# One decoder layer on one core: experts 0 and 1's rows selected in turned form, a ring of six raw weight tiles, and finer last pieces

## The reference

```python
y = mixer_sublayer(x, positions, w_in, w_branch_attn, w_branch_ret, w_out)
x = layer_norm(ALPHA * x + y, ln1_scale, ln1_bias)
y = hierarchical_moe(x, ...)          # top-1 group of 4, then top-2 of its 8 experts
x = layer_norm(ALPHA * x + y, ln2_scale, ln2_bias)
...
# one expert, for the rows that were routed to it
hid = silu(xb @ w_gate[e]) * (xb @ w_up[e])     # 2048 -> 512, twice
y = hid @ w_down[e]                             # 512 -> 2048
```

## Time and profile before

| | before |
|---|---|
| median of 3 runs | 2062.95 us (2062.85 to 2064.05) |
| the profiled execution's own time | 2060.22 us |
| its span, first to last instruction | 2058.1 us |
| TensorE busy | 1766.7 us, 86% |
| VectorE busy | 994.9 us, 48% |
| ScalarE busy | 757.1 us, 37% |
| mean granted clock | 0.928 |
| read from HBM | 609.61 MB |

### The profile page before, as it was taken

One profiled execution on the slowest core, in us unless ns is written; L12 is line 12 of the kernel. 1 busy time (PEld: TensorE's weight loads), 2 busy tenths in 40 slices (PEclk: granted clock), 3 DMA queues, 4 the chain that ended last, 5 costly groups with the idle time before them and its releaser, 6 DMA issues.

```text
span 2058.1 us, 25311 instructions
## 1 busy us (share of the span) xinstructions
PE 1766.7 (86%) x9868; PEld 1141.9 (55%) x9868; DVE 994.9 (48%) x1469; ACT 757.1 (37%) x1321; POOL 15.3 (1%) x34
## 2 busy tenths in 40 slices
PE   9999999999999999999999986666566666666667
PEld 7888888888888888888888541111112111111222
DVE  5454454555444444566565564334433433343357
ACT  5444444344444444354443422222222222222221
POOL 0000000000000000000000000000000000000000
PEclk9999999999999999999999988887888888887888
DMA  7556655455556555467677999999999999999998
GB/s 247 194 175 189 199 175 176 150 184 187 191 181 194 172 185 178 155 188 238 218 279 287 381 428 425 429 431 429 427 430 433 430 426 429 431 430 427 430 428 367
DMA packets 139042, 615.07 MB, mean 299 GB/s; under 512 B 14228, under 2 KB 14900, under 8 KB 117840
## 3 DMA queue, kind: packets, MB, share of 16 engines
q1 hardware_dynamic: 138240, 611.75, 77.5%
q0 software_dynamic: 720, 2.18, 0.6%
HBM read 609.61 MB, written 2.36 MB: 297 GB/s over the span
## 4 chain that ended last, share of the span: by engine, by line
PE 54%; DMA 33%; issue 10%; DVE 2%; ACT 0%; SPq 0%; DVEq 0%; POOL 0%; POOLq 0%
DMA W<-in_w_expert_up_dram 21%; PE PS L593 14%; PE PS L595 14%; PE PS L594 14%; DMA W<-in_w_expert_down_dram 11%; PE PS L1173 5%; PE PS L1224 2%; PE PS L962 1%; PE PS L1314 0%; PE PS L1129 0%; DVE ZACC L2234 0%; PE PS L1052 0%; DMA VC<-VS 0%; PE PS L1295 0%; PE PS L939 0%
## 5 line engine op out<-in xcount | busy, mean ns | idle before, releaser
L570 DVE TENSOR_TENSOR WL<-RAW,WH 128x1024 fp32r<-128x1024 f32 x384 | 457.4, 1221 | 403.9 <-ACT WH L566 402.5
L566 ACT ACTIVATE WH<-RAW 128x1024 fp32r<-128x1024 f32 x384 | 394.5, 1058 | 261.6 <-PE PS L595 199.8
L593 PE MATMUL PS<-WH,XH 128*128 128x512 f32 x1216 | 480.0, 395 | 0.1
L595 PE MATMUL PS<-WH,XL 128*128 128x512 f32 x1216 | 474.0, 390 | 0.0
L594 PE MATMUL PS<-WL,XH 128*128 128x512 f32 x1216 | 473.3, 389 | 0.0
L1173 PE MATMUL PS<-W,XE 128*32 128x512 f32 x2016 | 277.3, 698 | 135.0 <-DMA W<-in_w_expert_up_dram 133.6
L2234 DVE TENSOR_TENSOR ZACC<-PS,ZACC 128x1024 f32<-128x1024 f32 x124 | 146.0, 1219 | 294.3 <-PE PS L1295 294.3
L1224 PE MATMUL PS<-W,HT 128*32 128x512 f32 x992 | 171.0, 851 | 135.7 <-DMA W<-in_w_expert_down_dram 135.7
L593 PEld LDWEIGHTS PS<-WH,XH 128*128 128x128 f32 x1216 | 228.3, 188 | 49.3 <-issue 1.7
L595 PEld LDWEIGHTS PS<-WH,XL 128*128 128x128 f32 x1216 | 228.2, 188 | 48.3
L594 PEld LDWEIGHTS PS<-WL,XH 128*128 128x128 f32 x1216 | 228.6, 188 | 45.8
(11 more groups left out here) (333 smaller groups left out, 1472.7 us busy)
## 6 DMA issues: line engine op xcount, KB each, us to landing
RAW<-in_w_in_dram SPq DMA_DIRECT2D x304, 512.0 KB, 4.5
W<-in_w_expert_gate_dram SPq DMA_DIRECT2D x61, 2048.0 KB, 28.6
W<-in_w_expert_up_dram SPq DMA_DIRECT2D x61, 2048.0 KB, 33.0
W<-in_w_expert_down_dram SPq DMA_DIRECT2D x28, 4096.0 KB, 35.2
RAW<-in_w_branch_ret_dram SPq DMA_DIRECT2D x32, 512.0 KB, 5.2
RAW<-in_w_out_dram SPq DMA_DIRECT2D x32, 512.0 KB, 6.0
W<-in_w_expert_down_dram SPq DMA_DIRECT2D x7, 2048.0 KB, 30.4
RAW<-in_w_branch_attn_dram SPq DMA_DIRECT2D x16, 512.0 KB, 5.3
```

The lines of the kernel that those rows point to most:

```text
L566: act.activation(WH[:, i % RING], RAW[:, i % RING], ACT.Copy).then_inc(hi_done, 1)
L570: dve.tensor_tensor(WL[:, i % RING], RAW[:, i % RING], WH[:, i % RING].bitcast(F32), ALU.subtract).then_inc(lo_done, 1)
L593: pe.matmul(PS[:, bank + t], hs, wh, start=first and j == 0, stop=False)
L595: mm = pe.matmul(PS[:, bank + t], ls, wh, start=False, stop=end)
```

## The change

1. **Selection of items 0 and 1.** `gather` and `turn_rows` are no longer used for them. `gather_turned(k)` makes, for each of the 16 channel blocks k, two products (one per token tile) with 128 columns of ZN (every eighth column) as stationary operand and both items' selections, SEL01, 64 columns, as moving operand. The result is already turned. ScalarE scales it straight to XE of both items: 16 operations of 128 x 64 in place of 32 of 128 x 32 and two copies. XG0, XG1 and SEL1 are gone.
2. **TensorE's order.** Item 0's 16 places are done one by one, with a gather_turned two places ahead between them and, in the first half, item 1's place behind each.
3. **The ring.** RAW has six places, WL is written over RAW, and the load of tile n waits for `tile_used` of tile n - 6.
4. **Last pieces.** One piece of WT0 (1 MiB) is issued behind tile 27 of the output projection; the others are of 512 KB, each waiting for a pair of tiles; W11 moves up from the end.
5. `select_next(2)` on VectorE waits for all 16 turned products (`first_turned`) in place of gather(1).

```diff
 RING = 4
+RAWS = 6
...
-    RAW = at("RAW", 32, [RING, KT, CH])
-    WH = at("WH", 48, [RING, KT, CH], F32R)
-    WL = at("WL", 64, [RING, KT, CH], F32R)
+    RAW = at("RAW", 40, [RAWS, KT, CH])
+    WL = at("WL", 40, [RAWS, KT, CH], F32R)
+    WH = at("WH", 64, [RING, KT, CH], F32R)
...
-    def load_tile(eng, tile, i, src):
-
-        eng.wait_ge(lo_done, tile + 1)
-        eng.dma_start(RAW[:, i % RING], src).then_inc(raw_landed[i % RING], 16)
+    def load_tile(eng, tile, src):
+
+        if tile >= RAWS:
+            eng.wait_ge(tile_used, tile - RAWS + 1 + RING)
+        eng.dma_start(RAW[:, tile % RAWS], src).then_inc(raw_landed[tile % RAWS], 16)
...
+    def first_place(k):
+
+        return (XE_BANK, SPREAD + 1)[k % 2], k // 2 * 2 * ROWS
...
+            if n == 27:
+                load_apart(1, 4, 8)
...
-        sp.wait_ge(lo_done, T4 - 2 + RING)
-        load_apart(1, 4, 8)
+        sp.wait_ge(tile_used, T4 - 6 + RING)
+        load_apart(0, 0, 2)
         sp.wait_ge(tile_used, T4 - 4 + RING)
-        load_apart(0, 0, 4)
-        sp.wait_ge(tile_used, T4 - 1 + RING)
-        load_apart(0, 4, 7)
-        load_apart(1, 0, 3)
+        load_apart(0, 2, 4)
+        sp.dma_start(W11[:], gate_w[:, 1, 1, 0:2 * HID]).then_inc(part_landed, 16)
+        sp.wait_ge(tile_used, T4 - 2 + RING)
+        load_apart(0, 4, 6)
+        load_apart(1, 0, 2)
         sp.wait_ge(tile_used, T4 + RING)
-        load_apart(0, 7, 8)
-        load_apart(1, 3, 4)
+        load_apart(0, 6, 8)
+        load_apart(1, 2, 4)
         for c in range(2):
             load_block(0, 2, 2, c)
-        sp.wait_ge(lo_done, T4 + RING)
-        sp.dma_start(W11[:], gate_w[:, 1, 1, 0:2 * HID]).then_inc(part_landed, 16)
...
+        def gather_turned(k):
+
+            bank, c0 = first_place(k)
+            a = k // KQ * KQ * P + k % KQ
+            for t in range(TOK):
+                mm = pe.matmul(PS[:, bank, c0:c0 + 2 * ROWS], ZN[:, t, a:a + KQ * P - k % KQ:KQ],
+                               SEL01[:, t].rearrange("p i r -> p (i r)"), start=t == 0, stop=t == TOK - 1)
+            mm.then_inc(first_turned, 1)
...
-        gather(0)
+        pe.wait_ge(sel_ready, 2 * TOK)
+        pe.wait_ge(z_norm, TOK)
+        gather_turned(0)
+        gather_turned(1)
         place_rows()
-        turn_rows(0)
-        count_rows()
-        pe.wait_ge(sel_ready, 2 * TOK)
-        gate_up(0, 0, 0, take(0), gathered_between=1)
-        gate_up(1, 1, 0, take(1))
-        gate_up(0, 0, 1, take(0))
+        for k in range(KD):
+            q, j = divmod(k, KQ)
+            gate_up(0, 0, q, take(0), places=range(j, j + 1))
+            if k == 1:
+                count_rows()
+            if k + 2 < KD:
+                gather_turned(k + 2)
+            if q == 0:
+                gate_up(1, 1, 0, take(1), places=range(j, j + 1))
         gather(2)
         gate_up(1, 1, 1, take(1))
...
+        for k in range(KD):
+            act.wait_ge(first_turned, k + 1)
+            bank, c0 = first_place(k)
+            act.activation(XE[:, :, k], PS[:, bank, c0:c0 + 2 * ROWS].rearrange("p (i r) -> p i r", i=2), ACT.Identity,
+                           bias=LSB[:, 1, k:k + 1], scale=LSB[:, 0, k:k + 1]).then_inc(
+                *((xe_first, 1) if k < KD - 1 else (xe_stored, 2 * QS)))
...
-            dve.wait_ge(gathered, item)
+            if isinstance(item, int) and item == 2:
+                dve.wait_ge(first_turned, KD)
+            else:
+                dve.wait_ge(gathered, item - 2)
```

More of the change, by code:

```diff
@@ L471, in sem @@
         return ctx.enter_context(nc.semaphore(name))
-    raw_landed = [sem(f"raw_landed{i}") for i in range(RING)]
+    raw_landed = [sem(f"raw_landed{i}") for i in range(RAWS)]
     hi_done, lo_done, tile_used = sem("hi_done"), sem("lo_done"), sem("tile_used")
@@ L1120, in gather @@
             pe.wait_ge(sel_ready, item * TOK + TOK)
[L1121 to L1125 removed]
+            pe.wait_ge(xe_stored, item * QS)
             for t in range(TOK):
@@ L1149, in gate_up @@
                 pe.wait_ge(part_landed, 16 * 6)
-            for m in range(2):
+            for m in range(2) if places[0] == 0 else ():
                 if apart:
-                    pe.wait_ge(t_landed[m], 16 * 3)
+                    pe.wait_ge(t_landed[m], 16 * (4, 3)[m])
                 elif more:
@@ L1160, in gate_up @@
                     pe.wait_ge(w_landed[pair_q][1], item * 8 + (16 * loads_until(q, k4, (0, 1)) - 8 * k4))
-            for j in range(KQ):
+            for j in places:
                 k = KQ * q + j
                 odd = j % 2
-                if by_place and j < KQ - 1:
-                    pe.wait_ge(xe_first, item * (KQ - 1) + j + 1)
+                if by_place and k < KD - 1:
+                    pe.wait_ge(xe_first, k + 1)
                 elif by_place:
-                    pe.wait_ge(xe_stored, item * QS + 1)
+                    pe.wait_ge(xe_stored, 2 * QS)
                 for m in range(2):
@@ L1178, in gate_up @@
                         pe.wait_ge(late_landed[m], 16)
-                if gathered_between is not None and j % 2 and j < KQ - 1:
+                if isinstance(item, int) and item == 0 and q == 0 and odd and j < KQ - 1:
                     mm.then_inc(gu_part, 1)
-                    if j == 3:
-                        gather(gathered_between)
-                    elif j == 5:
-                        turn_rows(gathered_between)
-            mm.then_inc(gu_used, 2)
+            if places[-1] == KQ - 1:
+                mm.then_inc(gu_used, 2)
         def turn_hidden(item):
@@ L1588, in _ @@
         for n in range(BR):
[L1589 removed]
+            split_high(act, T2 + n, n)
             if n == LAG - 1:
```

77 lines of the change are left out of this document (29 added, 48 removed).

## The result

| | before | after |
|---|---|---|
| median | 2062.85 us (5 runs, 2061.11 to 2064.05) | **2084.31 us** (5 runs, 2079.82 to 2085.28) |
| ratio to before, 95% interval | | 1.0102 (1.0091 to 1.0114) |
| the profiled execution's time and span | 2060.22, 2058.1 us | 2083.52, 2081.5 us |
| mean granted clock | 0.928 | 0.927 |

The change costs 21.5 us by the medians. The forecast was +6.3 us, 2069.2, in a range that ended at 2076. The direction was right, the size was not.

A forecast was written before the change was run, and what follows sets the result against it. Experts' stage bound by DMA bytes: item 1's down block landing +5.7 us, plus 0.6 for TensorE's later loads, gave +6.3 on the profiled 2060.2; with 2.7 to the median, 2069.2 us, range 2061.5 to 2076.

The forecast's parts named there:

- The bound and the mark: Experts' stage lasts as long as its bytes take; the landing of item 1's down block, 1186.9 us, sets the end.
- The ring of six: Raw tiles in the mixer, issued 13.5 us before TensorE needs them: bounds 0 and +3 us, taken as 0.
- the pieces: Last loads before the mixer's last tile are out of the way sooner: gain 0 to 1 us, taken as 0.7.
- A pair of the new products between two groups: TensorE's selections of items 0 and 1: 0.70 us per visit, 0.21 of it the rest of the changeover, 14 visits.
- weight loads with every eighth column: Turned products' loads, named among things that would each add 2 to 7 us; XG's step of four was 0.12 us.
- Selections ready at 1149.22: Hand-over to the experts: selections for both items ready at 1149.22 us, TensorE's turned products starting at 1149.3.
- the third rival: Worse than forecast, chance 0.14: item places not running together, +13.2 us; dear weight loads, lower clock or ring waits, 2 to 7 each.
- ScalarE hidden by TensorE's groups: ScalarE's one 128 x 64 operation per 1.56 us step takes under 1.06 us, two pairs ahead, so it adds nothing.
- The empty queue gives back 2.9 us: Item 1's down block, issued 8.6 us later into an empty DMA queue, takes 12.7 us and lands only 5.7 later.
- VectorE's wait: VectorE's later hidden(0) holds TensorE's turn_hidden(0) to 1182.3 us, though TensorE is there at 1179.6: +0.6 us on the stream.
- No price for the changeover: Rival, chance 0.24: a turned pair's visit costs only its four weight loads, 0.44 us; +2.1 us, 2065.1.
- Everything hides: Rival, chance 0.10: turned products run in the groups' shadow, a step is 0.86 us; -2 us, 2061.

The follow-up runs named there:

- the run with the wait and no fall of the clock: The changed kernel with 128 columns of z side by side, not every eighth, as the turned products' stationary operand: 2073.20 us, ratio 1.0047.
- the run with the products apart: The changed kernel with its turned products in two runs of eight places ahead of all groups of the first halves, columns still every eighth: 2079.35 us, ratio 1.0077.
- the run with both edits: The changed kernel with turned products in two runs of eight places ahead of the groups, and stationary columns side by side: 2070.47 us, ratio 1.0041.
- the two without the wait: The changed kernel with select_next(2) behind DIAG and VAL, 2079.60 us; the same with side-by-side stationary columns and each moving column twice, 2071.62 us.

## Why the prediction missed

- **The bound and the mark: right.** The experts' stage was limited by its bytes before and after (1.01 share, 430 GB/s), and the time followed the landing of item 1's down block at a slope of 0.9 to 1.
- **The ring of six, 0, and the pieces, 0.7 us and lost again: right as far as the runs can tell.** 1.0003 and 0.9997, while 0.7 us is less than they resolve. One sign of being right, "TensorE's mixer without new gaps", did not hold: a wait of 0.8 us at 1075 us.
- **"A pair of the new products between two groups thus costs about 0.27 + 0.22 + 0.21 = 0.70 us": the step that failed.** It took 1.23, and the first two pairs 1.95 us in place of 0.93. Together 14 x 0.53 + 1.0 = 8.4 us, of which 8.1 are 64 loads of 0.238 us instead of 0.112. The term of the changeover was sized right, 0.73 for the visit with contiguous columns, though its 0.21 is not worked out in full: 0.31 less the 0.05 by which a first product is dearer would be 0.26. I had named "weight loads with every eighth column" among the things that would add 2 to 7 us, but took XG's turn for its price, "XG's step is four, 0.12 us". The row was of another kind of instruction. The bound from both sides should have had a doubled load in it, 4 x 0.12 x 16 = 7.7 us, and the range would then have ended some 8 us higher, near 2084.
- **Selections ready at 1149.22: 2.9 us later in this profile (1152.16, the first product at 1152.22).** 1.7 is the clock in the hand-over, 1.4 the mixer's end, and 0.2 came back. The first stands in two profiles with the kernel before's program up to there, and of the second up to 1.3. I had used the one profile of before as if it were typical, though it lay 2.7 us under its median.
- **The granted clock in the first groups: not priced.** From 1155.4 to 1158.8 us it was at the lower level, and two groups and the pair between them took 4.19 us (1154.93 to 1159.12) where later ones take 3.09: 1.1 us. It is in the third rival as a possibility.
- **ScalarE hidden by TensorE's groups: not at the end.** The last group took 1.29 us (1185.88 to 1187.17) and not 0.86, because the last place's weight load waited 0.48 us for ScalarE's XE. Item 1's second half to the issue took another 0.2 us more than its 3.4 + 0.25.
- **The empty queue gives back 2.9 us: too much.** 4 MiB took 13.6 us and not 12.7, so 2.0 came back. In the run with ten products added 0.7 did.
- **VectorE's wait: in place, and shorter than forecast (1.82 for 2.7 us).** I had +0.6 us on the stream for it. The landings show +2.4, but the run with the wait and no fall of the clock shows about 0.5. So its price was near, and the fall of the clock behind it was not in the sum.
- **The sum.** On the down block's issue: 8.4 (pairs) + 2.9 (start) + 1.1 (clock) + 0.4 (last group) + 0.2 (item 1's second half) = 13.0 against 21.4 - 8.6 = 12.8 measured. Then 0.9 (queue) and 1.8 (2.4 - 0.6, mostly the clock behind the wait). That makes 6.3 + 12.8 + 0.9 + 1.8 = 21.8 us at the last landings, where the profile has 21.9; the medians have 21.5, the profiled spans 23.4.
- **The rivals.** No price for the changeover: refuted. Ahead of a turned pair's loads stand 0.84 us of idle time wherever the pair follows a group at full clock, and a contiguous place takes 1.59 us where that rule made 1.30. The Trainium skill's sentence on weight loads pulled ahead ("TensorE: Matmul & The Clock Gate", section "Step-by-step: what each phase is for") comes with conditions, and it doesn't hold where 32 columns change to 128; "TensorEngine Tiling (Array Packing)", section "Key Properties", does, and the trace agrees. Everything hides: refuted. Pairs not running together: refuted, they start within 0.02 us of each other. Ring of six: not 2 to 7 us; the 0.8 us above is what can be seen of it. A lower clock: 1.7, 1.1 and some 1.8 us in this profile. What happened is the third rival in the part to which I gave least thought, with a whole chance of 0.14.

## What to carry to other kernels

Take the price of a weight load from a row of the same kind of instruction at the same distance of columns: an f32 product with columns four or more apart loads in twice the time, and a turn tells nothing of it. In a stage bound by its bytes, find the one load whose landing starts the whole stream and count only what TensorE does ahead of it; and when VectorE's work needs nothing from the wait ahead of it, move the wait behind (here the landings gained 3.0 us by it, the median nothing that can be told). A single profile can lie several us from its kernel's median, so look in it for what differs by chance (here a hand-over with the lower clock) before pricing from it.

## What the runs showed of the hardware

- The weight load of an f32 product of 128 columns: 0.112, 0.118, 0.175, 0.235 and 0.238 us from start to start for columns one, two, three, four and eight apart; of a turn about 0.1 at each distance.
- The dear load doesn't gain from the clock: in the run with the products apart it stayed at 0.238 us while the granted clock was 0.50, where contiguous loads, in the run with both edits, had gone from 0.112 to 0.214.
- A wait of TensorE of 1.82 us was followed within 2 us by 3.4 us at the lower clock in four of five profiles, 1.6 us more in the changed kernel's; the fifth kept the full clock, as did the two without the wait.
- The five filling products of the hand-over took 4.54 or 6.23 us, in profiles of either kernel.
